# A two-block network in one kernel: the squares, scales and last adds at the seams of the first block

## What is computed

```
h = modulate(rmsnorm(x, g1), shift, scale)      # entry 0: context and latent rows
x = x + gate * even_mixer(h)                    # seam 1 behind it
x = x + gate * peer(modulate(rmsnorm(x, g2)))   # experts, layer 0; seam 2 behind it
x = x + gate * mlstm(modulate(rmsnorm(x, g1)))  # seam 3 behind it
x = x + gate * peer(modulate(rmsnorm(x, g2)))   # experts, layer 1; seam 4 behind it
x = rmsnorm(x, norm_f)                          # block_norm, then the second block
```

## Time and profile before

| | us |
|---|---|
| median of 3 runs | 4228.78 |
| lowest, highest | 4223.34, 4234.53 |
| the profiled execution's own time | 4227.75 |
| its span | 4226.0 |
| DVE busy | 3330.0 (79%) |
| ACT busy | 2060.4 (49%) |
| POOL busy | 616.0 (15%) |

### The profile page before, as it was taken

How to read it: one execution, slowest core, us unless ns; L and a number is a source line. 1 busy time by engine, 2 the same in 40 slices (tenths; PEclk the granted TensorE clock), 3 DMA queues, 4 the chain that set the end, 5 groups by cost and what they waited for, 6 DMA issues and landing times. The chain is left out here.

```text
span 4226.0 us, 66651 instructions
## 1 busy us (share of the span) xinstructions
PE 3969.2 (94%) x23036; PEld 3502.0 (83%) x23036; DVE 3330.0 (79%) x7634; ACT 2060.4 (49%) x4043; POOL 616.0 (15%) x475
## 2 busy tenths in 40 slices
PE   7989999999999998989999999899989999988998
PEld 5568999989878886769999887688878888887887
DVE  7777999899778887668966677688676888867687
ACT  5334343577334444335567555444365544436544
POOL 0000034222222221001775000000002000000200
PEclk9999999999999999989999999999999999999999
DMA  6335488899999995657899888654445444544544
GB/s 245 105 135 178 156 301 297 273 295 293 367 340 355 355 348 186 231 179 231 218 233 246 280 277 279 199 193 171 126 130 195 169 179 181 178 131 131 195 169 150
DMA packets 409309, 939.84 MB, mean 222 GB/s; under 512 B 52282, under 2 KB 233770, under 8 KB 395450
## 3 DMA queue, kind: packets, MB, share of 16 engines
q1 hardware_dynamic: 353724, 801.85, 56.8%
q0 software_dynamic: 55296, 134.31, 9.9%
HBM read 842.60 MB, written 93.42 MB: 221 GB/s over the span
## 5 line engine op out<-in xcount | busy, mean ns | idle before, releaser
L167 DVE TENSOR_TENSOR w_low__2<-w_raw__2,w_high__2 128x512 fp32r<-128x512 f32 x544 | 361.6, 688 | 122.8 <-ACT w_high__2 L162 98.1
L162 ACT ACTIVATE w_high<-w_raw 128x512 fp32r<-128x512 f32 x576 | 343.0, 625 | 217.7 <-PE side L149 95.2
L167 DVE TENSOR_TENSOR w_low<-w_raw,w_high 128x512 fp32r<-128x512 f32 x576 | 381.7, 686 | 72.6 <-ACT w_high L162 71.1
L147 PE MATMUL hidden<-hT_high__2,w_high 128*128 128x384 f32 (+1 forms) x1280 | 424.8, 332 | 10.5 <-DVE w_low L167 6.7
L148 PE MATMUL hidden<-hT_low__2,w_high 128*128 128x384 f32 (+1 forms) x1280 | 420.1, 328 | 0.0
L149 PE MATMUL hidden<-hT_high__2,w_low 128*128 128x384 f32 (+1 forms) x1280 | 419.7, 328 | 0.0
L162 ACT ACTIVATE w_high__2<-w_raw__2 128x512 fp32r<-128x512 f32 x544 | 322.2, 624 | 115.5 <-DMA w_raw__2<-in_peer_v 59.3
L147 PE MATMUL hidden__3<-hT_high__4,w_high__2 128*128 128x256 f32 x1152 | 326.8, 284 | 0.0
L149 PE MATMUL hidden__3<-hT_high__4,w_low__2 128*128 128x256 f32 x1152 | 323.4, 281 | 0.0
L148 PE MATMUL hidden__3<-hT_low__4,w_high__2 128*128 128x256 f32 x1152 | 323.2, 281 | 0.0
L1161 POOL DMA_INDIRECT scattered_dram<-selected__3,routing_cells x128 | 230.9, 1804 | 158.0 <-DVE selected__3 L1513 94.0
(11 more groups left out here) (1060 smaller groups left out, 11754.9 us busy)
## 6 DMA issues: line engine op xcount, KB each, us to landing
w_raw<-in_peer_u SPq DMA_DIRECT2D x128, 512.0 KB
w_raw<-in_peer_v SPq DMA_DIRECT2D x128, 512.0 KB
w_raw__2<-in_peer_u SPq DMA_DIRECT2D x128, 512.0 KB
w_raw__2<-in_peer_v SPq DMA_DIRECT2D x128, 512.0 KB
carried_raw__2<-in_up SPq DMA_DIRECT2D x44, 1024.0 KB, 5.4
activated_dram<-activated SPq DMA_DIRECT2D x128, 192.0 KB
routing_dram<-routing SPq DMA_DIRECT2D x24, 1024.0 KB
routing_chunk<-routing_dram SPq DMA_DIRECT2D x16, 1536.0 KB
```

The costliest lines, as they stand in the source:

```text
L147: nc.tensor.matmul(out, lhs[0], rhs[0], start=start, stop=False, skip_group_check=True)
L162: return nc.scalar.activation(high, src, ACT.Copy)
L167: return nc.vector.tensor_tensor(low, src, high.bitcast(F32), ALU.subtract)
```

## The change

1. `RowSquares` is new. Where a stage has added a half row (tile, 512 columns) to the residual rows, ACT squares it in the same stage, into `row_squares` (128 x 4 x 2), ahead of the barrier; its output proper goes to a PSUM bank that has been read. The next stage's DVE adds the two halves (128x4 or 128x2) instead of waiting for `act_squares`. Entry 0 keeps its squares.
2. `NormIn` no longer scales rows. DVE multiplies the identity by each tile's inverse roots (128x128 a tile), and `pe_turn` multiplies the residual rows by that diagonal, with a plain product instead of a transpose. This holds for entry 0 and seams 1 to 3. `block_norm` keeps its scaling.
3. The last two down blocks of the experts go by column halves: left of 62, left of 63, right of 62, right of 63.
4. The adds go tile by tile, multiply and add, and in the last half each tile is released by its own last product (`last_tiles`). The gathered tile's add goes in two halves, between the left and the right half of the others.

```diff
@@ NormIn
+        self.diag = self.rows[:, 0, 0:self.n * P].rearrange("p (k t) -> p k t", k=self.n)
+        self.halves, self.steps = halves, 5 if halves is not None else 4
     def act_squares(self, act):
+        if self.halves is not None:
+            return
     def dve_scale(self, dve):
-        dve.wait_ge(self.summed, self.n)
+        if self.halves is not None:
+            part = self.halves[:, self.tiles[0]:self.tiles[-1] + 1, :]
+            chain.then(nc.vector.tensor_tensor(self.ss[:, :], part[:, :, 0], part[:, :, 1], ALU.add))
+        else:
+            dve.wait_ge(self.summed, self.n)
...
-            nc.vector.tensor_scalar(self.rows[:, k, :], self.xs[:, t, :], self.inv[:, k:k + 1], None, ALU.mult) \
+            nc.vector.tensor_scalar(self.diag[:, k, :], self.ident[:, :], self.inv[:, k:k + 1], None, ALU.mult) \
                 .then_inc(self.scaled, 1)
...
-                last = self.nc.tensor.transpose(self.banks[c % nb][:, k * P:(k + 1) * P],
-                                                self.rows[:, k, c * P:(c + 1) * P], self.ident[:, :])
+                last = self.nc.tensor.matmul(self.banks[c % nb][:, k * P:(k + 1) * P],
+                                             self.xs[:, t, c * P:(c + 1) * P], self.diag[:, k, :], start=True, stop=True)
+class RowSquares:
+    def __init__(self, nc, st, xs, halves, order):
+        self.nc, self.xs, self.halves, self.order = nc, xs, halves, order
+        self.final, self.squared = st.sem("rows_final"), st.sem("rows_squared")
+    def act_squares(self, act, scratch):
+        for k, (t, i) in enumerate(self.order):
+            act.wait_ge(self.final, k + 1)
+            if k:
+                act.wait_ge(self.squared, k)
+            self.nc.scalar.activation(scratch(t, i), self.xs[:, t, i * 512:(i + 1) * 512], ACT.Square,
+                                      accum_out=self.halves[:, t, i:i + 1]).then_inc(self.squared, 1)
+        act.wait_ge(self.squared, len(self.order))
@@ experts
-            for d in range(DOWN):
-                combine(d)
+            for d in range(DOWN - 2):
+                for n in range(2):
+                    combine_half(d, n)
+            for n in range(2):
+                for d in range(DOWN - 2, DOWN):
+                    combine_half(d, n)
...
+                    if n == 1 and t < ND - 1:
+                        dve.wait_ge(last_tiles, t + 1)
+                    else:
+                        dve.wait_ge(used, 2 * SLOTS - (2 if n == 0 else 0))
+                    chain.wrote(nc.vector.tensor_tensor(bank(n, t), bank(n, t), gate[:, t // TT, part], ALU.mult))
+                    chain.settle()
+                    nc.vector.tensor_tensor(xs[:, tiles[t], part], xs[:, tiles[t], part], bank(n, t), ALU.add) \
+                        .then_inc(squares.final, 1)
@@ even_mixer (mlstm alike)
             def add_rows(i):
-                dve.wait_ge(pieces.used, OUT + KC * (i + 1))
                 part = slice(i * 512, (i + 1) * 512)
                 for t in range(4):
+                    if i == 0 or t == 3:
+                        dve.wait_ge(pieces.used, OUT + KC * (i + 1))
+                    else:
+                        dve.wait_ge(last_tiles, t + 1)
                     chain.wrote(nc.vector.tensor_tensor(v[:, t, :], (acc, bank)[i][t][:, :],
                                                         gates[:, 1 if t < 2 else 0, part], ALU.mult))
-                chain.settle()
-                for t in range(4):
-                    last = nc.vector.tensor_tensor(xs[:, t, part], xs[:, t, part], v[:, t, :], ALU.add)
-                last.then_inc(done, 1)
-                dve.wait_ge(done, i + 1)
+                    chain.settle()
+                    nc.vector.tensor_tensor(xs[:, t, part], xs[:, t, part], v[:, t, :], ALU.add) \
+                        .then_inc(squares.final, 1)
@@ block_norm
-            for k, t in enumerate(tiles):
+            for k, t in enumerate(tiles if halves is None else ()):
```

More of the change, by code:

```diff
@@ L170, with __init__ @@
 class NormIn:
-    def __init__(self, nc, st, ident, xs, tiles, spans, high, low, banks, hT=None, rows=None, tmp=None):
+    def __init__(self, nc, st, ident, xs, tiles, spans, high, low, banks, hT=None, rows=None, tmp=None, halves=None):
         self.nc, self.ident, self.xs, self.tiles, self.spans = nc, ident, xs, tiles, spans
@@ L1223, in route, with combine_half @@
                 last.then_inc(product, 1)
-            def combine(d):
+            def combine_half(d, n):
                 s = UP + d
                 pe.wait_ge(weighed_split, d + 1)
[L1228 to L1238, removed]
+                pe.wait_ge(split, 2 * s + n + 1)
+                if d == 0:
+                    pe.wait_ge(staged_in, NG)
+                    pe.wait_ge(evacuated, UP)
+                part = slice(n * 512, (n + 1) * 512)
+                for t in range(ND):
+                    cut = slice(t * P, (t + 1) * P)
+                    last = three_products(nc, bank(n, t), (w_high[:, d % 2, cut], w_low[:, d % 2, cut]),
+                                          (high[:, s % RB, part], low[:, s % RB, part]), d == 0, d == DOWN - 1)
+                    if d == DOWN - 1 and n == 1 and t < ND - 1:
+                        last.then_inc(last_tiles, 1)
+                last.then_inc(used, 1)
             normed.pe_turn(pe, turn_back if items else None)
@@ L1380, in _ @@
                     angles.act_sines(act)
+            squares.act_squares(act, lambda t, i: bank(i, tiles.index(t)) if tiles.index(t) < ND else bank(0, 0))
         @block.vector
@@ L1790, in even_mixer @@
         normed = NormIn(nc, st, *norm, h_high, h_low, bank, None, rows, moved)
+        squares = RowSquares(nc, st, xs, halves, [(t, i) for i in range(2) for t in range(4)])
+        last_tiles = st.sem("last_tiles_ready")
         side = SideProducts(nc, st, modulate, jobs, ring[:, :, :], (silu[:, 0, :], silu[:, 1, :]), junk[:, :])
@@ L2126, in _ @@
                 pieces.act_high(act, n + AHEAD)
+            squares.act_squares(act, lambda t, i: (acc, bank)[i][t][:, :])
         @block.vector
@@ L2348, in mlstm @@
         bank = [st.psum(f"chain{r}", [P, 512]) for r in range(4)]
-        normed = NormIn(nc, st, *norm, h_high, h_low, bank, None, rows, moved)
+        normed = NormIn(nc, st, *norm, h_high, h_low, bank, None, rows, moved, halves)
+        squares = RowSquares(nc, st, xs, halves, [(2 + k, i) for i in range(2) for k in range(TT)])
+        last_tile = st.sem("last_tile_ready")
         b_loaded, pick_loaded, gate_loaded = (st.sem(x) for x in ("b_loaded", "sel4_loaded", "gate_row_loaded"))
@@ L2819, in _, with first_block @@
             add_rows(1)
-            dve.wait_ge(done, 2)
-def first_block(nc, outer, ident, consts, cols, w, xs, mod_rows, spilled, routed, loads, later):
+            squares.dve_done(dve)
+def first_block(nc, outer, ident, consts, cols, w, xs, mod_rows, spilled, routed, loads, later, halves):
     N = 2 * T
@@ L3923, in second_block, with block_norm @@
     carried.close()
-def block_norm(nc, xs, gain, out=None, hand=None):
+def block_norm(nc, xs, gain, out=None, halves=None, hand=None):
     tiles = (2, 3)
@@ L3981, in _ @@
             chain = Chain(dve, own)
-            dve.wait_ge(summed, n)
+            if halves is None:
+                dve.wait_ge(summed, n)
+            else:
+                chain.then(nc.vector.tensor_tensor(ss[:, :], halves[:, tiles[0]:tiles[-1] + 1, 0],
+                                                   halves[:, tiles[0]:tiles[-1] + 1, 1], ALU.add))
             nc.vector.tensor_scalar(mean[:, :], ss[:, :], 1.0 / D, EPS, ALU.mult, ALU.add).then_inc(meaned, 1)
```

90 lines of the change are left out of this document (52 added, 38 removed).

## The result

The changed kernel is slower: 4243.39 us in the median of 20 runs (4235.03 to 4252.36), against 4228.36 for 20 runs of the kernel before beside it. The ratio is 1.0038, 95% interval 1.0030 to 1.0045, or 13 to 19 us. The forecast was 4229 and no measurable change; 4243 lies outside its range. The profiled execution took 4243.92 us, with a span of 4242.2.

What follows compares the result with a forecast made beforehand. PE holds 94% of the span, so only four seams between stages and entry 0 can move, where POOL's clears open the inverse root. Terms of +1.5 and -1.2 us gave +0.3, so a median of 4229 us, range 4218 to 4241.

Steps and rivals of the forecast that it cites:

- the gathers or the loads: Outside the four seams and entry 0: held untouched; a difference over 13 us placed there would show the prediction wrong.
- rival B: Entries with turns: plain turns run at the low clock throughout, the rise later than some 8 us; 4243 us, chance 0.12.
- (a): Four seams: squares ahead of the barrier gain 0 behind POOL's clears; new tail +0.8 us, more clears +0.14 us a seam.
- (b): Adds by tiles and down blocks by column halves: +0.4, -0.75, -0.55 and -1.37 us at seams 1 to 4.
- Rival A: Seams: ACT's squares were the bound after all, so the whole of them would go; near 4217 us, chance 0.08.
- (c): Entry 0, seams 1 to 3: DVE writes diagonals, 0.9 us for 2.74; together with (d) -1.2 us.
- (d): Turns as plain products, slower at low clock; with (c) entry 0 -0.3, seams 1 to 3 -1.5, +0.5, +0.1 us.
- C: Entries with turns: the clock rises early, 3.3 us after the first plain product; 4227 us, chance 0.2.
- save 1.6 us: Seam 1: denser PE raises the clock inside the turns, so the first products, until now at low clock, save 1.6 us.

Runs made afterwards that it cites:

- e1: The kernel before with an unused buffer of 32 bytes a partition, moving all later left-side buffers by 32 bytes: 4238.71 us, ratio 1.0016.
- e11: The kernel before with the unused 32 bytes at the upper end of memory, moving only the carried buffers: 4241.10 us, ratio 1.0024.
- e13: The kernel before with 112 unread 2-column transposes (224 PE instructions), half at entry 0, half at seam 1: 4239.44 us, ratio 1.0017.
- e5: The changed kernel with row_squares at the upper end of memory, so that no other buffer's address moves: 4234.56 us, ratio 1.0010 to the kernel before.
- e18: The changed kernel, its buffer left in place, with 16 unread transposes at entry 0: 4237.42 us, ratio 1.0016 to the kernel before.
- e17: The kernel before with the unused 32-byte buffer and the 112 unread transposes, none of the change: 4242.79 us, ratio 1.0031.
- e6: e5 with POOL's semaphore clears moved behind the power of the norm: 4219.00 us, ratio 0.9977 to the kernel before.
- e7: The kernel before with POOL's clears moved behind the power of the norm, squares still behind the barrier: 4224.53 us, ratio 0.9983.

## Why the prediction was wrong

The step that failed is the one that the last paragraph named as what would make it wrong: "the gathers or the loads, which I hold to be untouched", and with them the second block. It got no term in the sum, since no instruction of it changes. But a program is also a layout of buffers and a stream of code. Put into the kernel before, the shift by 32 bytes costs 1.0016 and 1.0024 (e1, e11) and the 112 unread transposes cost 1.0017 (e13); taken out of the changed one, the shift gives back 0.0028 (e5) and the moved fetches 0.0022 (e18). That is 7 to 12 us and 7 to 9 us, and both together (e17: 1.0031) make the result. That the second of the two works by the place of PE's code fetches is likely and not proven. No rival had either; rival B came near 4243 for another reason.

The prediction's terms themselves are not what failed, but for one. Parts (a) and (b), from the start of PE's last product to the start of the power, in us:

| seam | before | after | measured | forecast |
|---|---|---|---|---|
| 1 | 11.30 | 12.92 | +1.62 | +1.3 |
| 2 | 12.02 | 12.00 | -0.02 | +0.2 |
| 3 | 7.90 | 8.18 | +0.28 | +0.4 |
| 4 | 10.33 | 9.75 | -0.58 | -0.4 |

Sum +1.3 for +1.5.

- **(a), the squares and the clears:** right. Gain 0, DVE's root waiting 4.7 to 5.9 us for POOL at all four seams, the last half row's square 0.60 us and its read 0.19. Rival A is out: with early clears there was nothing to take, and e6 and e7 show what takes it.
- **(b), the adds:** right; with (a), every seam within 0.3 us.
- **(c) and (d), diagonals and plain turns:** right at entry 0 (-0.2 for the -0.3 forecast) and, from the root's end to the last split, at seam 3 (8.9 us now, 8.86 before); at seam 2 the +0.5 did not come (13.99 for 13.96). The turns were 0.21 us a record before the rise and 0.10 after it, as taken, and the rise came 4.1, 4.9 and 4.1 us after the first plain product at entry 0 and seams 2 and 3, against rivals B and C. Seam 1 failed: from the root's end to the last split it takes 18.3 us where it took 17.7, so +0.6 for the -1.5 forecast. The clock did rise inside the turns, but only 9.1 us after the first of them, past the 8 us of rival B, and it fell again when they had gaps, so the first products ran at the low level as before (stretch, length, busy times, then granted clock):

```profile
320.00:323.00 3.00, 3.00 (x15) 2.81 (x14) 1.29 (x3) 1.02 (x2) 0.00 (x0) 0.50 0.00 0
323.00:326.00 3.00, 1.93 (x15) 1.64 (x15) 2.20 (x5) 2.56 (x5) 0.00 (x0) 0.88 0.00 0
...
334.00:337.00 3.00, 3.00 (x16) 3.00 (x16) 1.57 (x4) 2.84 (x4) 0.00 (x0) 0.50 0.67 198
```

The step was that the first products "save 1.6 us"; here the clock was back at the low level when they ran. The terms come to +0.5 in place of -1.2 for (c) and (d), and to +1.8 us in place of +0.3 in all: too little to explain 15.

The first block's 8 us in the profiled pair are not explained by these terms and are probably scatter: its longest stage, the experts of layer 0, takes 1345 to 1360 us over the profiles in no order that follows the edits.

The Trainium skill ("SBUF — State Buffer", Operand start alignment) says where an operand may start and adds that this is "about legality, not speed". That sentence is no contradiction, but the runs add the speed: 390 against 398 ns. And the Trainium skill ("Trainium Architecture — The Big Picture", The software stack) has instruction streams moved into the engines' memory when a program is loaded. That sentence speaks of loading alone; here the trace shows 2.65 MB in 162 packets of the kind "instruction" on q8 during the execution.

## What to carry to other kernels

Before costing an edit at nothing outside its stages, ask what it moves for everybody: the address of every later buffer, and the number of instructions ahead of every later stage. Compare a group's median duration and the stages' lengths in parts that the edit doesn't touch, and put new small buffers where nothing shifts. And where a chain of short steps opens with a step that waits for nothing and still starts late, look at that engine's queue: here bookkeeping hid the whole gain of the squares, and moving it gave 12 to 20 us.

## What the runs showed of the hardware

- The gated layers' 128x512 fp32 product took 390, 398 or 392 ns in the median as the distance of its two operands in the partition was that of before, 32 bytes more, or 64 more; its weight load took 188 ns in all. What in the memory or its ports makes this is open.
- What I take for PE's code came in packets of 16 KB, one every 255 instructions in the median, during the execution. Chains with such a packet among their first loads took 220.1 us in the mean, those without 223.6. It helped here; elsewhere it need not.
- A semaphore's clear took 0.074 to 0.077 us of POOL's queue and is in no busy time: 63 of them, 4.8 us.
